# Gate and up weights of a mixture of experts in f16 halves, double-buffered, with each partition's weights read in one run

## What is computed

```python
def expert_block(args):                      # xb: 128 rows x 1024, e: its expert
    xb, e = args
    return (jax.nn.silu(xb @ w_g[e]) * (xb @ w_u[e])) @ w_d[e]     # w_g, w_u: 1024 x 512, w_d: 512 x 1024

y = ybuf.reshape(n_blocks * MOE_BLK, D_MODEL)[dest] * gate_s[:, None]
return jax.ops.segment_sum(y, tok_s, num_segments=n_tok)
```

## Time and profile before

| what | value |
|---|---|
| median of 3 runs | 2752.8 us (2750.51 to 2752.84) |
| the profiled execution | 2750.93 us, span 2749.3 us |
| mean granted clock of TensorE | 0.987 of full |
| instructions | 49924, of them 14252 matmuls |
| HBM traffic | 309.74 MB read, 87.88 MB written |
| mixer | to about 1316 us |
| expert stage | from about 1316 us |

### The profile page before, as it was taken

How to read it: one execution, slowest core, us unless ns; L and a number is a source line. 1 busy time by engine, 2 the same in 40 slices (tenths; PEclk the granted TensorE clock), 3 DMA queues, 4 the chain that set the end, 5 groups by cost and what they waited for, 6 DMA issues and landing times.

```text
span 2749.3 us, 49924 instructions
## 1 busy us (share of the span) xinstructions
PE 2643.6 (96%) x14252; PEld 1820.9 (66%) x14253; DVE 1716.2 (62%) x3920; ACT 1391.3 (51%) x3046; POOL 798.8 (29%) x825
## 2 busy tenths in 40 slices
PE   4999999999999999996699999999999999999997
PEld 2455555555555555553588888888888888888886
DVE  5677777777777777776454455545655444546633
ACT  7666555565555566553344445445545333435533
POOL 1122323232322222331232333323223323333232
PEclk9999999999999999998799999999999999999999
DMA  8376555556655555656556677667767665667763
GB/s 315 82 166 166 156 160 158 152 157 165 163 152 160 154 156 164 166 138 167 187 169 189 186 236 244 200 196 224 235 186 232 205 183 153 194 180 237 235 181 54
DMA packets 546395, 495.22 MB, mean 180 GB/s; under 512 B 411787, under 2 KB 411948, under 8 KB 545340
## 3 DMA queue, kind: packets, MB, share of 16 engines
q1 hardware_dynamic: 517516, 406.08, 49.2%
q0 software_dynamic: 28848, 88.77, 13.8%
HBM read 309.74 MB, written 87.88 MB: 145 GB/s over the span
## 4 chain that ended last, share of the span: by engine, by line
PE 89%; DVE 3%; DMA 3%; ACT 2%; issue 1%; SPq 1%; POOL 1%; POOLq 0%; DVEq 0%; ACTq 0%
PE psB L1676 15%; PE psA L1676 15%; PE psG L574 11%; PE psF L1676 7%; PE psG L1676 7%; PE psE L574 6%; PE psF L574 6%; PE psD L574 6%; PE psC L574 6%; PE psH L574 3%; PE psC L1684 1%; PE psD L1684 1%; PE psE L1691 1%; DMA xg<-hn_rows,slots 1%; DMA slots<-slot_table 1%
## 5 line engine op out<-in xcount | busy, mean ns | idle before, releaser
L574 PE MATMUL psG<-wi_all,both_xT 128*128 128x512 f16 x1536 | 345.2, 382 | 10.9 <-DMA both_xT<-x 10.9
L574 PEld LDWEIGHTS psG<-wi_all,both_xT 128*128 128x128 f16 x1536 | 148.7, 98 | 188.2 <-DMA both_xT<-x 11.1
L1600 POOL DMA_INDIRECT xg<-hn_rows,slots x80 | 99.2, 1240 | 544.0 <-DMA slots<-slot_table 389.4
L1676 PE MATMUL psB<-up_hi,gT_hi 128*128 128x512 f32 x632 | 254.4, 402 | 0.0
L1676 PE MATMUL psA<-gate_hi,gT_hi 128*128 128x512 f32 x632 | 247.3, 391 | 3.1 <-ACT gT_hi L1796 1.7
L1812 DVE TENSOR_TENSOR down_lo<-wi_all,down_hi 128x512 fp32r<-128x512 f32 x256 | 157.0, 686 | 147.1 <-ACT down_hi L1770 147.1
L1676 PE MATMUL psB<-up_hi,gT_lo 128*128 128x512 f32 x632 | 247.6, 392 | 0.0
L1676 PE MATMUL psA<-gate_hi,gT_lo 128*128 128x512 f32 x632 | 247.3, 391 | 0.0
L1676 PE MATMUL psA<-gate_lo,gT_hi 128*128 128x512 f32 x632 | 247.0, 391 | 0.0
L1676 PE MATMUL psB<-up_lo,gT_hi 128*128 128x512 f32 x632 | 246.4, 390 | 0.0
L1796 ACT ACTIVATE gT_hi<-psC 128x512 fp32r<-128x512 f32 x80 | 47.8, 597 | 384.8 <-PE psC L1684 384.8
(11 more groups left out here) (320 smaller groups left out, 5777.2 us busy)
## 6 DMA issues: line engine op xcount, KB each, us to landing
wi_all<-in_w_gate SPq DMA_DIRECT2D x32, 2048.0 KB, 9.5
wi_all<-in_w_up SPq DMA_DIRECT2D x32, 2048.0 KB, 12.9
wi_all<-in_w_down SPq DMA_DIRECT2D x32, 2048.0 KB, 11.7
xt<-in_x SPq DMA_DIRECT2D x32, 512.0 KB, 3.7
um<-u_rows SPq DMA_DIRECT2D x64, 256.0 KB, 2.7
out_rows<-h SPq DMA_DIRECT2D x32, 512.0 KB, 3.0
xres<-in_x SPq DMA_DIRECT2D x31, 512.0 KB, 4.1
hn_rows<-xres SPq DMA_DIRECT2D x31, 512.0 KB, 2.9
```

The lines of the kernel that those rows point to most:

```text
L574: m = nc.tensor.matmul(ps, left[:, l, k, :], weights.half(r, k, n, width), start=(k == opens and j == 0), stop=(k == closes and j == 2))
L1600: pool.indirect_dma_start(xg[:], None, hn_dram, bass.IndirectOffsetOnAxis(ap=slots[:, 0, 0:1], axis=0), bounds_check=SEQ + P - 1).then_inc ...
L1676: m = nc.tensor.matmul(ps[:, :], l[:, k, :], r[:, r_k[n], :], start=(n == 0 and j == 0), stop=(n == len(l_k) - 1 and j == 2))
```

## The change

Gate and up get f16 halves in two copies (`hi[n][p]`, p = 0, 1), used by experts in turn; down keeps one pair in f32r. Gate and up also get two raw places each, so five raw places in all, and the load for expert e + 2 is issued when the split of expert e is done. f16 halves need a scale: ScalarE sums the absolute values of each partition's 4096 weights (`sum_next`), GpSimd takes the maximum over the partitions (`bound_of`), and VectorE makes a power of two and its inverse from it in five small steps (`scales`). The inverse is applied in `silu` and `product`. The rows are scaled by `hn_scale`, which the mixer already has.

The order changes. Sums of the next expert's weights are made in a first block, the scales and splits of gate and up of the next expert in the second block, and the split of down in the first. Splits come in 2 pieces of 2048 columns instead of 8 of 512. Every expert now has at least two blocks. In the walk the first two blocks are written out and the loop over experts takes two at a time.

The loads now put rows `p * 8 + k` on partition p, so that a partition's weights are one run of 16 KB. To match it the transposes take every eighth (rows) or every fourth (activations) column.

```diff
         def load_expert(sp, n, e, p):
             w = {"gate": w_gate, "up": w_up, "down": w_down}[n]
-            sp.dma_start(dst, w[0, bass.ds(e, 1)].rearrange("o (k p) n -> p (o k) n", p=P)).then_inc(raw_in[n], 16)
+            sp.dma_start(raw[n][p].rearrange("p k n -> p (k n)"),
+                         w[0, bass.ds(e, 1)].rearrange("o (p k) n -> p (o k n)", p=P)).then_inc(raw_in[n][p % len(raw_in[n])], 16)
...
-        step(v.tensor_scalar(blocks_of[:, counts], blocks_of[:, E:], 1, None, ALU.max))
-        step(v.tensor_scalar(blocks_of[:, 0:1], blocks_of[:, 0:1], 2, None, ALU.max))
+        step(v.tensor_scalar(blocks_of[:, counts], blocks_of[:, E:], 2, None, ALU.max))
...
-    hi = {n: sb(f"{n}_hi", [P, 8, 512], F32R) for n in raw}
-    lo = {n: sb(f"{n}_lo", [P, 8, 512], F32R) for n in raw}
+    SCALED = ("gate", "up")
+    hi = {n: [sb(f"{n}_hi_{p}", [P, 8, 512], F16) for p in range(2)] for n in SCALED}
+    lo = {n: [sb(f"{n}_lo_{p}", [P, 8, 512], F16) for p in range(2)] for n in SCALED}
+    hi["down"], lo["down"] = ([sb(f"down_{w}", [P, 8, 512], F32R)] * 2 for w in ("hi", "lo"))
-    gT_hi, gT_lo = sb("gT_hi", [P, KD, P], F32R), sb("gT_lo", [P, KD, P], F32R)
+    gT_hi, gT_lo = sb("gT_hi", [P, KD, P], F16), sb("gT_lo", [P, KD, P], F16)
...
     def sync(sp):
+        def next_loads(e, p, down=True):
+            for n in SCALED:
+                split_up(n, e)
+                load_expert(sp, n, e + 2, p)
+            if down:
+                split_up("down", e)
+                load_expert(sp, "down", e + 1, p)
+        sp.wait_ge(summed, 2)
+        for n in SCALED:
+            load_expert(sp, n, 1, 1)
         mixed(sp)
...
+        def bound_of(e, p):
+            pool.wait_ge(summed, 2 * (e + 1))
+            hold(pool, held)
+            pool.partition_all_reduce(most(p), sums(p), P, RMAX).then_inc(most_s, 1)
...
+            if isinstance(i, int) and i == 1 and not last:
+                bound_of(e + 1, 1 - p)
...
-                    m = nc.tensor.transpose(ps[:, c * P:(c + 1) * P], xg[:, (4 * h + c) * P:(4 * h + c + 1) * P], ident)
+                    m = nc.tensor.transpose(ps[:, c * P:(c + 1) * P], xg[:].rearrange("t (p k) -> t k p", k=KD)[:, 4 * h + c, :], ident)
-                m = nc.tensor.transpose(psE[:, c * P:(c + 1) * P], act_rows[:, c * P:(c + 1) * P], ident)
+                m = nc.tensor.transpose(psE[:, c * P:(c + 1) * P], act_rows[:].rearrange("t (p k) -> t k p", k=KE)[:, c, :], ident)
...
+        def block_(e, i, b, p, r, last):          # ScalarE
+            if not (known and b < 2):
+                copy_y(b)
+            if not (known and b == 0):
+                turn(b)
+            silu(b, p)
+            if first and not last:
+                sum_next("gate", p, r, b)
+            if second and not last:
+                split("gate", e + 1, 1 - p)
+            turn_x(b + 1)
+            if first and not last:
+                sum_next("up", p, r, b)
+            if first:
+                split_down(e, b)
+            if second and not last:
+                split("up", e + 1, 1 - p)
...
+        def block_(e, i, b, p, r, last):          # VectorE
+            if not (known and b < 2):
+                copy_y(b)
+            if second and not last:
+                scales(e + 1, 1 - p)
+            if not (known and b == 0):
+                turn(b)
+            if second and not last:
+                split("gate", e + 1, 1 - p)
+            product(b, p)
+            turn_x(b + 1)
+            if first:
+                split_down(e)
+            if second and not last:
+                split("up", e + 1, 1 - p)
```

More of the change, by code:

```diff
@@ L363, in mixer @@
     last = sig("last").sem
-    planned = 18
+    planned = 17
     LAST = TILES
@@ L1562, in experts @@
     named = sem("named")
[L1564 to L1585, removed]
@@ L1587, in sync, with walk, expert @@
-    def sync(sp):
-        mixed(sp)
[L1590 to L1594, removed]
+    SCALE_STEPS = 5
+    def walk(eng, block):
+        def expert(e, p, r, last=False):
+            n = eng.value_load(blocks_of[0:1, bass.ds(e, 1)], min_val=2, max_val=TILES)
+            base = eng.value_load(blocks_of[0:1, bass.ds(e + E, 1)], min_val=0, max_val=4 * TILES)
+            start = 0 if isinstance(e, int) and e == 0 else base
+            block(e, 0, start, p, r, last)
+            block(e, 1, start + 1, p, r, last)
+            with eng.If(n > 2):
+                with eng.Fori(2, n) as i:
+                    block(e, i, start + i, p, r, last)
+            return base + n
+        expert(0, 0, 0)
+        with eng.Fori(0, (E - 2) // 2) as pair:
+            expert(pair * 2 + 1, 1, pair)
+            expert(pair * 2 + 2, 0, pair + 1)
+        return expert(E - 1, 1, (E - 1) // 2, True)
@@ L1782, in silu @@
                 act.wait_ge(act_s, b)
-            s.activation(gated[:], psA[:, :], ACT.Silu).then_inc(silu_s, 1)
+            s.activation(gated[:], psA[:, :], ACT.Silu, scale=inverse(p, "gate")).then_inc(silu_s, 1)
         def turn(b):
@@ L1799, in scalar, with scales, step @@
         s.preload_act_table_set("silu_and_others")
+        for c, n in enumerate(SCALED):
+            sum_up(n, 0, 0, wi_flat[:, 12288 + c * 2048:12288 + (c + 1) * 2048].bitcast(BF16))
         mixed(act)
         act.sem_inc(y_act, 3)
-        halves(act, split, copy_y, silu, turn, turn_x)
+        split("gate", 0, 0)
+        turn_x(0)
+        split("up", 0, 0)
+        total = walk(act, block_)
+        copy_y(total)
+        turn(total)
+        copy_y(total + 1)
     def vector(dve):
         v = nc.vector
-        def split(n, e):
-            dve.wait_ge(raw_in[n], 16 * (e + 1))
-            for k in range(8):
-                dve.wait_ge(hi_s[n], e * 8 + k + 1)
-                v.tensor_tensor(lo[n][:, k, :], raw[n][:, k, :], hi[n][:, k, :].bitcast(F32),
-                                ALU.subtract).then_inc(lo_s[n], 1)
+        def scales(e, p):
+            dve.wait_ge(most_s, e + 1)
+            done = [0]
+            def step(ins):
+                done[0] += 1
+                ins.then_inc(step_s, 1)
+                dve.wait_ge(step_s, SCALE_STEPS * e + done[0])
+                hold(dve, held)
+            bits, floor = own[:, p, 4:6].bitcast(I32), own[:, p, 6:8].bitcast(I32)
+            step(v.tensor_scalar(bits, most(p).bitcast(I32), 0x7F800000, None, ALU.bitwise_and))
+            step(v.tensor_scalar(floor, bits, float(30 << 23), None, ALU.max))
+            step(v.tensor_scalar(power(p).bitcast(I32), floor, -1.0, float(268 << 23), ALU.mult, ALU.add))
+            step(v.tensor_scalar(inverse(p).bitcast(I32), floor, float(-(14 << 23)), None, ALU.add))
+            step(v.tensor_scalar(inverse(p), inverse(p), inv_hn, None, ALU.mult))
+            assert done[0] == SCALE_STEPS
@@ L1845, in vector @@
         dve.sem_inc(y_dve, 3)
-        halves(dve, split, copy_y, product, turn, turn_x)
+        split("gate", 0, 0)
+        turn_x(0)
+        split("up", 0, 0)
+        total = walk(dve, block_)
+        copy_y(total)
+        turn(total)
+        copy_y(total + 1)
     return dict(sync=sync, tensor=tensor, scalar=scalar, gpsimd=gpsimd, vector=vector)
```

162 lines of the change are left out of this document (96 added, 66 removed).

## The result

The changed kernel takes 2946.9 us (median; the kernel before, measured beside it, 2752.8): ratio 1.069, 95% interval 1.065 to 1.074, slower. The forecast was 2737 and its range ended at 2805. The profiled execution has a span of 2932.6 us, 183.3 more than before.

What follows compares the result with a forecast made beforehand. The prediction took TensorE's own instructions as the bound (busy 96% of the span) and summed 2750.9 - 41 + 0 + 9 + 15 + 3 = 2737 us, with a range of 2710 to 2805.

Steps and rivals of the forecast that it cites:

- Number of blocks: Expert stage: the floor of two blocks per expert adds no block to the 79, cost 0.
- f16 halves: Gate and up matmuls: 48 of 72 in a block become f16, each 0.0109 us shorter, gain 41 us.
- Stepped transposes: Twelve TensorE transposes a block, reading columns with a step: taken as 0, upper end +108 us.
- Rival B: The stepped column reads of the transposes are slow: 2821 us, or 2767 with half the cost; chance 0.25.
- Sums and scales: ScalarE and VectorE, second block (start T): gT_lo late for the next gate by 0.3 us, 9 us for 31 experts.
- GpSimd and its queue: All-reduce ahead of slot load and gather, timed from S, the first block's start: gather in time, 0, bound 1.1 us.
- The step on loads: 96 weight loads of 2 MB in longer pieces: gate and up have an expert's time in advance, landing changes hidden.
- The gather behind the gate load: Next gather, about two us into the block, meets the gate load: 0.5 us for 31 experts, +15, bounds 0 and 56.
- Start: Before the first block: expert 1's loads come earlier and meet the first gather, +3 us.
- Rival C: GpSimd's copies, and the slot load, held by VectorE's coarse pieces: 2 us per expert, 2784 us; chance 0.22.

Runs made afterwards that it cites:

- e10: e1 with four pieces a split instead of two, plus e9's two waits in SyncE's queue: 2723.2 us.
- e11: e10 with the short runs (2 and 4 KB) and contiguous transposes of the kernel before: 2719.6 us.
- e4: The kernel before with only the long runs of 16 KB and the stepped transposes: 2766.0 us.
- e1: The changed kernel with ScalarE's two sums earlier in the first block: 2752.4 us.
- e9: The changed kernel with two waits in SyncE's queue, so the up and down loads are issued only when the gather in front has landed: 2742.5 us.
- e5: e1 with the first loads of expert 1 held until the all-reduce of expert 0: 2763.3 us.
- e8: e1 with expert 1's loads held behind the first all-reduce, four pieces a split, short runs and contiguous transposes: 2769.4 us.

## Why the prediction was wrong

Step by step, as the prediction put them:

- *Number of blocks*, 79: right (632 matmuls of each kind).
- *f16 halves*, 41 us: right. 24 gate matmuls take 5.19 us (2045.73 to 2050.92), 5.18 was forecast, and e10 is 41.9 us shorter than the kernel before from the first gate matmul on.
- *Stepped transposes*, 0: right within 4 us (e11 against e10), though e4 leaves up to 13 us for steps and long runs together. Rival B is out: it needed 0.03 us a transpose to decide, and the means moved by 0.009 us at most. The rule of the Trainium skill, "SBUF — State Buffer" (Door 1: The DMA port swizzle), that each crossing to a new 16-byte line pays a penalty, was weighed there; no more of it than these 0.009 us shows in the transposes.
- *Sums and scales*, 9 us for gT_lo: right in e1 and e9 (9.7 and 9.5 us) and mostly hidden in the kernel after by its longer blocks (2.9), as the text said it would be.
- *GpSimd and its queue*: **the step that failed.** It put the gather's issue at S+21 to 24.6, and it came at S+22.8. It gave it "landing 4.5 us later" and took 0 with a bound of 1.1 us. The landing was 10.6, because the split of down, placed by the same text at T+6.7 = S+24, releases the down load just then. The step on loads counted only whether the loads were in time, and the start of the down load was never set beside that of the gather. The row that gave the price of a collision was there: 9.58 us. With it, S + 22.8 + 9.58 is 4.4 us behind the due S+28; measured are 5.1 to 5.6 us, at each expert with two blocks (14 from 1400 to 2700 us, 74.2 us of waits).
- The gather behind the gate load, "by 1.8 us at most too late", +15 with bounds 0 and 56: 23 gathers ended behind the up load instead. Nine of them, at experts with three blocks, made TensorE wait 3.4 to 5.9 us each; all 23 took 45.9 us. The sum is inside the bounds, but by another load and at a third of the experts, so that is luck.
- *The clock behind a stall* was in no term: some 60 of the 66 us by which TensorE is busy longer, two fifths of the waits' own size.
- *Start*, 3 us: 12.0 (first gate matmul at 1341.85; 10.1 in e10). The prediction looked for a collision and left out the all-reduce, which now stands ahead of the first slot load with a gap of 7.6 us before it. Some 3 us of that gap go with the two weight loads in flight (e5, e8); the rest is unexplained.
- Rival C had the sign and the engine (GpSimd's chain late), but its mechanism, copies held by coarse pieces, and its 2 us per expert were wrong: the copies took 0.19 us in the median and over 0.5 us in 9 of 154; what was held was the gather's own instruction, and the price was 5.2 us and 2.0 of half clock.

## What to carry to other kernels

When GpSimd and SyncE both issue transfers, write the times of their issues side by side for each block: a gather whose instruction ends even 0.8 us behind the issue of a 2 MB load landed here only some 9 us after that issue, about when the load does. If the load has slack, let it wait for the gather; two such waits were worth 197 us here. Look at the end of the gather's instruction, not at its start: beside VectorE it took 2 to 4 us instead of 1.07, and the same end of VectorE let the load go. A stall of TensorE cost more than its length here: add the half clock that followed (2 us behind 5).

## What was not expected of the hardware

- A gather lands in 4.4 us by itself, and in 11.0 us if a load with runs of 16 KB was issued 0.8 us before its instruction ended (9.8 with 2 and 4 KB); the landing falls to 7.7 us at 2.3 us and 6.4 at 4.9 us. 1 KB of slots cost GpSimd 7.4 us right behind the issue of a load (e5), and 4.0 with the last load issued 9 us before (e1).
- Halving VectorE's pieces made GpSimd's hold longer (4.2 us instead of 2.0), and copies of 0.19 us took up to 1.5 in e10 and 2.3 in the kernel after.
- The first all-reduce after a long pause has 6.9 to 9.6 us ahead of it in which the profile shows nothing, wherever it stands, with weight loads in flight, and 4.0 to 4.2 us with none. That is what the rows show; no run tells why.
